# A transformer kernel on one core: turns ahead of the key products, keys in other banks, and another order inside the modulation chains

## The reference

```python
x_lat = x_lat + g2_l * rmsnorm(swiglu(f_l, w_gate[l], w_up[l], w_down[l]), norm_ffn_post[l])
...
# next layer
h_l = rmsnorm(x_lat, norm_mix_pre[l]) * (1.0 + sc1_l) + sh1_l
h_c = rmsnorm(x_ctx, norm_mix_pre[l]) * (1.0 + sc1_c) + sh1_c
q_l, k_l, v_l, z_l, xbc_l, dt_l = jnp.split(h_lat @ w_in, IN_SPLITS, axis=-1)
...
xbc = depthwise_conv_silu(xbc, conv_w, conv_b)
```

## Time and profile before

| | us |
|---|---|
| median of three runs | 2770.21 (2768.75 to 2771.43) |
| profiled execution | 2772.69 |
| its span, first to last instruction | 2771.4 |
| TensorE busy | 2620.0 (95%) |
| VectorE busy | 2125.7 (77%) |
| ScalarE busy | 1486.9 (54%) |
| GpSimd busy | 110.6 (4%) |
| mean granted TensorE clock | 0.969 |

### The profile page before, as it was taken

How to read it: one execution, slowest core, us unless ns; L and a number is a source line. 1 busy time by engine, 2 the same in 40 slices (tenths; PEclk the granted TensorE clock), 3 DMA queues, 4 the chain that set the end, 5 groups by cost and what they waited for, 6 DMA issues and landing times.

```text
span 2771.4 us, 32200 instructions
## 1 busy us (share of the span) xinstructions
PE 2620.0 (95%) x12954; PEld 2132.0 (77%) x12954; DVE 2125.7 (77%) x2511; ACT 1486.9 (54%) x1665; POOL 110.6 (4%) x145
## 2 busy tenths in 40 slices
PE   7989998998998889999999999999999999999997
PEld 4767676887777678877788777788888888888886
DVE  4555566787647657868688667799999999999997
ACT  4332364445443244344633526677667776767674
POOL 4023100000000300000000000000000000000000
PEclk9999899999999989999999999999999999999999
DMA  7543545885553036952289340599999999999994
GB/s 277 183 156 122 190 166 191 299 304 203 180 210 122 1 121 240 327 197 95 96 305 328 136 175 31 185 371 364 351 367 368 353 362 365 362 354 367 369 364 189
DMA packets 290442, 675.24 MB, mean 244 GB/s; under 512 B 16726, under 2 KB 113158, under 8 KB 271344
## 3 DMA queue, kind: packets, MB, share of 16 engines
q1 hardware_dynamic: 285152, 664.35, 65.9%
q0 software_dynamic: 4272, 7.72, 1.1%
q10 hardware_dynamic: 864, 1.06, 0.1%
HBM read 671.98 MB, written 1.10 MB: 243 GB/s over the span
## 4 chain that ended last, share of the span: by engine, by line
PE 76%; DVE 13%; ACT 7%; DMA 2%; issue 1%; SPq 0%; POOL 0%; ACTq 0%; DVEq 0%; POOLq 0%
PE psum L553 21%; PE psum L555 21%; PE psum L554 21%; PE psum L76 7%; DVE wslot_r L563 3%; PE psum L1524 1%; PE psum L396 1%; ACT whi_r L76 1%; PE psum L1663 1%; DVE cacc L76 1%; PE psum L3063 1%; DVE dslot_r L563 1%; DMA first<-in_w_mod 1%; PE psum L2091 1%; DVE x L76 1%
## 5 line engine op out<-in xcount | busy, mean ns | idle before, releaser
L553 PE MATMUL psum<-whi_r,xhi_r 128*128 128x512 f32 (+1 forms) x752 | 295.5, 393 | 12.0 <-DVE wslot_r L563 5.4
L563 DVE TENSOR_TENSOR wslot_r<-wslot,whi_r 128x2048 fp32r<-128x2048 f32 (+1 forms) x114 | 255.6, 2252 | 61.5 <-ACT whi_r L76 61.1
L555 PE MATMUL psum<-whi_r,xlo_r 128*128 128x512 f32 (+1 forms) x752 | 290.4, 386 | 0.0
L554 PE MATMUL psum<-wslot_r,xhi_r 128*128 128x512 f32 (+1 forms) x736 | 283.7, 385 | 0.0
L76 ACT ACTIVATE whi_r<-wslot 128x2048 fp32r<-128x2048 f32 (+1 forms) x114 | 212.6, 1878 | 50.8 <-DMA wslot<-in_w_up 19.5
L563 DVE TENSOR_TENSOR wslot_r<-wslot,arena_r 128x2048 fp32r<-128x2048 f32 x85 | 194.0, 2288 | 18.7 <-ACT arena_r L3022 18.1
L563 DVE TENSOR_TENSOR ring_r<-ring,wide_r 128x2048 fp32r<-128x2048 f32 x84 | 191.8, 2288 | 17.8 <-ACT wide_r L3022 16.6
L563 DVE TENSOR_TENSOR wslot_r<-wslot,wide_r 128x2048 fp32r<-128x2048 f32 x83 | 189.7, 2288 | 16.7 <-ACT wide_r L3022 16.3
L563 DVE TENSOR_TENSOR ring_r<-ring,arena_r 128x2048 fp32r<-128x2048 f32 x84 | 191.6, 2287 | 11.6 <-ACT arena_r L3022 10.8
L3022 ACT ACTIVATE arena_r<-wslot 128x2048 fp32r<-128x2048 f32 x85 | 162.3, 1917 | 68.6 <-PE psum L555 45.6
L3022 ACT ACTIVATE arena_r<-ring 128x2048 fp32r<-128x2048 f32 x84 | 160.5, 1918 | 69.3 <-PE psum L555 48.5
(11 more groups left out here) (540 smaller groups left out, 6334.5 us busy)
## 6 DMA issues: line engine op xcount, KB each, us to landing
wslot<-in_moe_w_gate SPq DMA_DIRECT2D x29, 2048.0 KB, 8.0
ring<-in_moe_w_down SPq DMA_DIRECT2D x29, 2048.0 KB, 8.3
dot<-in_w_dots SPq DMA_DIRECT2D x112, 512.0 KB, 6.1
wslot<-in_moe_w_up SPq DMA_DIRECT2D x28, 2048.0 KB, 8.5
ring<-in_moe_w_up SPq DMA_DIRECT2D x28, 2048.0 KB, 8.8
ring<-in_moe_w_gate SPq DMA_DIRECT2D x27, 2048.0 KB, 8.2
wslot<-in_moe_w_down SPq DMA_DIRECT2D x27, 2048.0 KB, 8.1
dslot<-in_w_mod SPq DMA_DIRECT2D x42, 1024.0 KB, 4.8
```

The costliest lines, as they stand in the source:

```text
L553: t.matmul(out_, hi, w_hi, start=start, stop=False)
L554: t.matmul(out_, hi, w_lo, start=False, stop=False)
L555: return t.matmul(out_, lo, w_hi, start=False, stop=stop)
L563: return v.tensor_tensor(one_pass(lo), src, one_pass(hi), ALU.subtract)
```

## The change

In `onward`, a chain with a single set, two different banks and a `hi` tile goes to a new function `modulated`: all eight transposes stand in one run; ScalarE modulates half 1 and rounds it before anything of half 0; VectorE modulates half 0, then ScalarE rounds half 0; VectorE subtracts half 1 and then half 0. The product waits for the last subtraction, as before.

Behind the first loop, c0's turns and ScalarE's share of it are issued ahead of c1's second norm, the rest of c0 ahead of `next(mixers)`; one explicit piece of modulation stands there instead of three. In `joint_in(1)`, the four `KV` products use banks 4, 5, 6 and 4 and don't advance `nb`; `X0_` is split after the yield ahead of `KV` tile 2, not after tile 3; `step_sizes` runs after `KV` tile 3, not after `X0_` tile 0; the five dummies ahead of `X0_` are gone.

```diff
@@ onward
         yield "turn"
+        if len(sets) == 1 and banks[0] != banks[1] and sets[0][1] is not None:
+            yield from modulated(s, tt, temp, normed, *sets[0], banks, ready, t0, busy)
+            return
...
+    def modulated(s, tt, temp, normed, which, hi, lo, banks, ready, t0, busy):
+
+        c_, bks, halves, turned = cols_for[which], [], [slice(4 * half, 4 * half + 4) for half in range(2)], {}
+        for half, b in enumerate(banks):
+            bks.append(bank_for_pe(b))
+            if half == 0:
+                keep_busy(b, busy)
+            pe.wait(normed[half])
+            for k in range(4):
+                turned[half] = pe.free(t.transpose, bks[half][:, k * P:(k + 1) * P], temp[:, 4 * half + k:D:KD], ident[:])
+        for k in range(4, KD):
+            of_act = ac.put(a.activation, lo[:, k], bks[1][:, (k - 4) * P:(k - 3) * P], ACT.Identity, scale=c_[:, s, 0, k:k + 1],
+                            bias=c_[:, s, 1, k:k + 1], after=[turned[1]])
+        read_by(banks[1], of_act)
+        second = ac.put(a.activation, one_pass(hi[:, halves[1]]), lo[:, halves[1]], ACT.Copy, after=[of_act])
+        yield "half"
+        for k in range(4):
+            of_dve = ve.put(v.tensor_scalar, lo[:, k], bks[0][:, k * P:(k + 1) * P], c_[:, s, 0, k:k + 1], c_[:, s, 1, k:k + 1],
+                            ALU.mult, ALU.add, after=[turned[0]])
+        read_by(banks[0], of_dve)
+        first = ac.put(a.activation, one_pass(hi[:, halves[0]]), lo[:, halves[0]], ACT.Copy, after=[of_dve])
+        ve.put(low, lo[:, halves[1]], lo[:, halves[1]], hi[:, halves[1]], after=[second])
+        yield "late"
+        ready[which, t0 + tt] = ve.put(low, lo[:, halves[0]], lo[:, halves[0]], hi[:, halves[0]], after=[first])
@@ second_layer
             if j == KV:
                 if p_ == 3:
-                    split_tile(X0_)
+                    step_sizes()
             elif j == X0_:
-                if p_ == 0:
-                    step_sizes()
@@ product
             b = nb % 4
-            nb += 1
+            if l == 1 and j == KV:
+                b = (4, 5, 6, 4)[p_]
+            else:
+                nb += 1
...
-            keep_busy(b, {(0, X0_, 0): 9, (1, X0_, 0): 5, (1, Z_, 2): 6}.get((l, j, p_), 0))
+            keep_busy(b, {(0, X0_, 0): 9, (1, Z_, 2): 6}.get((l, j, p_), 0))
...
                 if l == 1 and j == KV and p_ == 2:
                     yield
+                    split_tile(X0_)
@@ behind the first line
+    to(c1, "normed")
+    to(c0, "half")
     to(c1, "turn")
     gate_read()
+    finish_off(c0)
     next(mixers)
-    finish_off(c0)
-    for _ in range(3):
-        mod_step()
+    mod_step()
     finish_off(c1)
```

## The result

On one chip the kernel before took 2769.48 (median of 4 runs, 2768.56 to 2771.43) and the changed kernel 2742.79 (4 runs, 2742.53 to 2749.40): 26.7 less, a ratio of 0.9895 with a 95% interval of 0.9871 to 0.9918. The changed kernel was measured twice more, beside the experiments: 2750.04 against 2777.68 (0.9900, 0.9883 to 0.9916) and 2747.37 against 2777.91 (0.9890, 0.9870 to 0.9911). So the gain was 26.7, 27.6 and 30.5 in the three comparisons. The forecast was 2746.8 with a gain of 23.4; the time of 2742.79 lies inside the range of 2740.5 to 2756.5, near its lower end, and the gain is 3.3 larger than forecast. The profiled execution of the changed kernel took 2742.65 with a span of 2741.3.

What follows compares the result with a forecast made beforehand. The convolution chain on VectorE and ScalarE bounds the stage from `X0_` to the attention, through `conv(0)`'s start. Stage 18.1 plus other chains 5.3 make 23.4; 2770.2 - 23.4 = 2746.8, range 2740.5 to 2756.5.

Steps and rivals of the forecast that it cites:

- part 3: Chains of the output stages and second feed-forward loop end earlier with halves side by side: 5.3 less together.
- term for the first output stage: At 379.46 TensorE's wait of 1.74 for a split queued behind c1's second rounding goes: 1.7 less.
- What bounds the stage: From `X0_` to the attention, the convolution chain on VectorE and ScalarE sets the time; the start of `conv(0)` matters.
- TensorE becomes the bound: Rival: moved pieces and product tiles hold the convolution back; stage gains 11.5 instead of 18.1, time 2753.4, chance 0.14.
- Parts 1 and 2: Behind the first loop: earlier transposes, other banks, two pieces fewer; earlier `X0_` split and `step_sizes`; `conv(0)` 18.2 earlier, stage 18.1.
- 0.1 off for the query and gate tiles: Late in the stage, TensorE's waits for query and gate splits take up its smaller gain: 18.1 instead of 18.2.
- The dummies at nothing: Ahead of `X0_`, removing five dummies (2.43) was costed at 0 beyond what the earlier start already counts.
- the two displaced pieces cost nothing: Two modulation pieces move to later `fill` calls, 1.0 of TensorE each; their later bias row, store and transposes costed at nothing.
- The rival of two switches at double price: Around `step_sizes`' exponential and logarithm, two table switches cost 2.6 more: gain 20.8, time 2749.4, chance 0.05.
- the lower bound: For the other chains: each of 5 could cost 0.6, as ScalarE starts behind eight transposes, not four; -3 in all.
- The clock phase: Rival: at 910 to 1000 the attention meets another clock phase, 6 us either way, 2741 to 2753, chance 0.13.
- the two upper bounds: Largest gains allowed: 20 for the stage behind the first loop, 8 for the other chains.

Runs made afterwards that it cites:

- dummies_x1: The changed kernel with eight more dummy products ahead of `X1_` tile 2: 2750.41, ratio to before 0.9929; stage time 103.34 against 102.86.
- dummies_x0: The changed kernel with the five dummies ahead of `X0_` tile 0 put back: 2752.21, ratio to before 0.9902; stage time 104.46 against 102.86.
- old_banks: The changed kernel with the four key tiles in banks 0 to 3 again: 2752.05, ratio to before 0.9933; stage time 113.00 against 102.86.
- split_back: The changed kernel with the `X0_` split behind key tile 3 again: 2742.05, ratio to before 0.9894; stage time 105.40 against 102.86.

## Where the prediction was right, and which step of it failed

**The step that failed** is part 3, the other chains, in its term for the first output stage. The sum had 1.7 there, the length of the wait of 1.74 at 379.46. Measured are 2.05 in that stage and 1.4 behind it, 3.45: with the old order a stretch near 424 runs at half clock, with the new one at full clock, and the sum put that at nothing. The places that can be read (without the sparse attention's input) sum to 6.95 where the prediction had 4.9 for them, and 1.75 of the 2.05 between these is this term. The mechanism, chains that end earlier where TensorE waits for them, was right.

**What bounds the stage** was right: the convolution chain on VectorE and ScalarE, with TensorE a few us ahead (`dummies_x1`). The rival *TensorE becomes the bound* priced a moment that `dummies_x1` shows to be some 3 us away; only at tiles 0 and 1 of `X0_` is it near (`dummies_x0`).

**Parts 1 and 2** can be compared time by time; the changed kernel's times are put on the axis of the prediction by adding 5.9.

| start of | forecast | measured |
|---|---|---|
| c0's transposes | 789.4 | 789.4 |
| c1's transposes | 798.5 | 798.0 |
| `KV` tile 2 | 799.9 | 799.8 |
| `KV` tile 3 | 803.8 | 803.9 |
| first `X0_` subtraction | 804.6 | 804.2 |
| `X0_` tile 0 | 807.7 | 808.0 |
| `conv(0)` | 815.8 | 815.5 |

The stage gave **18.8** where 18.1 was forecast. Of the 0.7, 0.3 is there by `conv(0)`, since the `X0_` subtractions begin 0.4 earlier than the sum had them. The other 0.4 is the tail. The prediction took 0.1 off for the query and gate tiles. VectorE's subtractions for them start 24.4 earlier, just as `conv(0)` does (866.66 to 842.29, 884.01 to 859.63), so nothing was lost there; and 0.3 more was won behind the key transposes, which before ran at half clock behind a longer wait (1.94 for eight, now 1.07):

```profile
895.54 1.94 PE L76 MATMUL psum<-c_ident,kdup 128*128 128x128 f32 x8 [3.44 <-DVE kdup L76]
```

The dummies at nothing were right as far as the start; putting them back costs 1.6. That the two displaced pieces cost nothing is supported: no idle bracket stands at any later piece of the stage, and the stage kept its gain.

**The parts don't add up singly.** The prediction summed along one chain of waits, and the single undoings show why only that way works: 4.75 + 10.14 + 10.44 + 5.35 + 2.54 = 33.2 for five of the parts, while all of them together give 18.8 and the chain order alone gives 0. The parts stand in line; each that is missing puts its own wait back at the end.

**The table switches.** The rival of two switches at double price is wrong. Between exponential and logarithm lie 0.07 and 0.01 around a load of 1.28 (804.85 to 804.92, 806.20 to 806.21), and from the `kvd` copies to `conv(0)` it is 6.85 where the sum had 6.7. The Trainium skill ("ScalarE: Activation LUTs", What ACT_TABLE_LOAD costs) puts a drain of 1.38 beside the load; the trace has none around that load, and none ahead of the one at 808.48, which starts 0.02 behind a copy (807.86 and 0.60). The measurement decides for 1.28.

**The rest of part 3.** The second output stage was forecast at 2.0 and gave 1.9; the sparse attention's output 1.2 and 1.6 (0.7 behind c0's chain and 0.9 behind c1's). At its input, forecast 0.4, the profile has 1.8, of which the repeats of one program show up to 1.6 to be clock, so it is left out of the 6.95 (with it forecast, part 3 was 5.3). No chain cost the 0.6 of the lower bound.

**The clock phase** was given +-6 with a chance of 0.13. It also sets the lower end of the range (2740.8); the two upper bounds by themselves give 2770.2 - 28 = 2742.2. In the other kernels the attention was between 4.2 shorter and 3.2 longer than in the changed kernel; against the kernel before the changed kernel's is 1.55 longer. Sum of what is attributed: 18.8 + 6.95 - 1.55 = 24.2, 0.8 over the forecast. That it comes so near is in part luck: the two terms were 2.35 too small, and the attention took 1.55 back that the sum had at nothing. The medians say 26.7, and the spans 30.1. Of the 5.9 that the spans have more, 2.4 lie ahead of 362, in code that the change doesn't touch; 1.8 at the sparse attention's input; and 1.5 between 1550 and 1600, also in untouched code, where other profiles lose up to 4.1. One program differs from itself by up to 2.05 and 1.6 at the first two of these places, and by 4.55 at 1300. So the 2.5 of the medians over the attributed sum isn't attributed to the change, and its cause stays open; with runs as few as these it isn't excluded that the change tilts one of those places.

**Not tried**: what makes the clock fall on one side or the other in the attention and at 1300. The order behind the loop, c0's turns ahead of the key products, was never undone by itself, so that part's own price isn't known: the trace shows c0's transposes start 8.1 earlier within the stage, and `old_banks` shows what they need of the banks.

## What to carry to other kernels

Where several small waits stand in line between two sublayers, removing one of them may show nothing: find the last one that would be left, and undo the parts one at a time from the finished version, not from the old one. Give a product a bank that the chain beside it doesn't need next. Put a filler that waits for a transfer only where its data have landed. Round weights on ScalarE ahead of an instruction that waits for VectorE. When a wait goes, look some tens of us behind it too, for a half-clock stretch that may go with it. Compare by the time between two landmarks in the trace where the change is a per cent of the whole, since the clock gives and takes several us elsewhere.

## What the runs showed of the hardware that was not expected

The stage repeats to 0.02 us over three executions of one program (102.86, 102.88, 102.86) with a full clock, while 30 us of unchanged code at 1290 take 4.55 more or not, at a granted clock of 0.61 or 0.85. A bank choice can cost 7.95 in one wait. In one profile a stage that is 2.54 slower (`split_back`) is followed by an attention that is 4.2 shorter at a higher granted clock. And a wait of 1.74 ahead of one product is followed, some 45 us later, by a half-clock stretch worth 1.4, in both profiles that have the wait and in none of the twelve that don't.
